# Loading the first FFN's weights as f32 through staging slots, with ScalarE and VectorE doing the cast

## What is computed

```python
def swiglu(h, w_gate, w_up, w_down):
    return (jax.nn.silu(h @ w_gate) * (h @ w_up)) @ w_down

x = x + 0.5 * swiglu(rmsnorm(x, ffn1_norm), ffn1_w_gate, ffn1_w_up, ffn1_w_down)
h = rmsnorm(x, mix_norm)
...
x = x + merged @ w_out
x = x + 0.5 * swiglu(rmsnorm(x, ffn2_norm), ffn2_w_gate, ffn2_w_up, ffn2_w_down)
```

## Time and profile before

| | |
|---|---|
| median of 3 runs | 3398.79 us |
| profiled execution | 3418.33 us |
| span on its slowest core (core 6) | 3416.7 us |
| spans of the 8 cores | 3388.2 to 3416.7 us |
| TensorE busy | 3075.1 us, 90% |
| VectorE, ScalarE, GpSimd busy | 33%, 26%, 20% |
| first matmul | 130.47 us |
| DMA moved | 403 MB, 118 GB/s on average |

### The profile page before, as it was taken

How to read it: one execution, slowest core, us unless ns; L and a number is a source line. 1 busy time by engine, 2 the same in 40 slices (tenths; PEclk the granted TensorE clock), 3 DMA queues, 4 the chain that set the end, 5 groups by cost and what they waited for, 6 DMA issues and landing times.

```text
span 3416.7 us, 41299 instructions; the slowest of 8 cores (3388.2 to 3416.7 us)
## 1 busy us (share of the span) xinstructions
PE 3075.1 (90%) x14115; PEld 1406.9 (41%) x14400; DVE 1115.5 (33%) x1555; ACT 893.4 (26%) x1733; POOL 690.1 (20%) x1149
## 2 busy tenths in 40 slices
PE   0487999898899879998999989999999999999999
PEld 0243444343344434443444444444444444444444
DVE  1111221121122464535365545453422221222111
ACT  0111111111111245363644353646221111111100
POOL 2000000000000463535244535342110000000000
PEclk9998999999999999999999999999999999999999
DMA  9743532632631648767578877656773212321111
GB/s 176 144 61 77 114 50 65 119 53 67 127 63 70 160 101 197 154 170 153 145 176 208 176 180 167 169 139 171 242 229 87 72 41 61 87 71 41 49 50 37
DMA packets 335976, 403.05 MB, mean 118 GB/s; under 512 B 208800, under 2 KB 217120, under 8 KB 335008
## 3 DMA queue, kind: packets, MB, share of 16 engines
q1 hardware_dynamic: 323248, 347.27, 39.2%
q0 software_dynamic: 12528, 53.12, 11.4%
HBM read 355.38 MB, written 86.64 MB: 129 GB/s over the span
## 4 chain that ended last, share of the span: by engine, by line
PE 74%; DMA 14%; SPq 3%; DVE 3%; POOL 3%; issue 2%; ACT 1%; another core or an unknown queue 0%; ACTq 0%; DVEq 0%; POOLq 0%
PE banks L698 74%; SPq L841 2%; DMA x1s<-axr_99 2%; DMA axr_98<-x 2%; DMA xin_68<-x 1%; DMA hT_66<-xn_71 1%; DMA xin_69<-x1s 1%; DMA x1s<-axr_98 1%; POOL hr L1030 1%; DMA KT<-kf 1%; DMA xin_69<-x 1%; POOL qf L1041 1%; SPq L869 1%; DMA QT_115<-qf 1%; DMA axr_99<-x 1%
## 5 line engine op out<-in xcount | busy, mean ns | idle before, releaser
L834 POOL TENSOR_SCALAR ssq<-ssq 128x1 f32<-128x1 f32 x96 | 19.4, 202 | 1645.5 <-ACT xn_70 L832 1544.1
L698 PE MATMUL banks<-awd,aact 128*128 128x512 bf16 x1380 | 304.4, 379 | 1.5
L698 PE MATMUL banks<-cwd,cact 128*128 128x512 bf16 x1380 | 303.7, 379 | 1.5
L698 PEld LDWEIGHTS banks<-cwd,cact 128*128 128x128 bf16 x1408 | 137.7, 98 | 166.2
L698 PEld LDWEIGHTS banks<-awd,aact 128*128 128x128 bf16 x1408 | 137.8, 98 | 165.6
L883 ACT ACTIVATE asg_94<-banks 128x512 f32<-128x512 f32 x88 | 52.6, 597 | 512.8 <-PE banks L698 499.7
L698 PE MATMUL banks<-hT_66,agu_72 128*128 128x512 bf16 x64 | 21.9, 518 | 166.4 <-DMA hT_66<-xn_71 130.5
L883 ACT ACTIVATE csg_161<-banks 128x512 f32<-128x512 f32 x88 | 52.5, 597 | 434.0 <-PE banks L698 433.9
L698 PE MATMUL banks<-QT_115,KT 128*128 128x512 bf16 (+3 forms) x377 | 131.5, 355 | 16.2 <-ACT pt_118 L1096 5.2
L1096 ACT ACTIVATE pt_118<-banks 128x512 bf16<-128x512 f32 (+2 forms) x216 | 115.9, 537 | 87.6 <-PE banks L698 84.0
L885 DVE TENSOR_TENSOR cact<-csg_162,banks 128x512 bf16<-128x512 f32 x88 | 60.5, 688 | 238.4 <-PE banks L698 224.6
(11 more groups left out here) (406 smaller groups left out, 5497.7 us busy)
## 6 DMA issues: line engine op xcount, KB each, us to landing
wms<-ws POOLq DMA_DIRECT2D x33, 512.0 KB, 6.7
ring_129<-wms SPq DMA_DIRECT2D x52, 256.0 KB, 4.3
ring_131<-wms SPq DMA_DIRECT2D x51, 256.0 KB, 3.8
ring_133<-wms SPq DMA_DIRECT2D x51, 256.0 KB, 4.0
ring_135<-wms SPq DMA_DIRECT2D x51, 256.0 KB, 4.1
ring_137<-wms SPq DMA_DIRECT2D x51, 256.0 KB, 3.8
ring_130<-wms SPq DMA_DIRECT2D x39, 256.0 KB, 4.7
ring_132<-wms SPq DMA_DIRECT2D x39, 256.0 KB, 4.9
```

The source lines that it names most:

```text
L698: fns.append(lambda e, o_=o_, l_=l_, r_=r_, st=st, sp_=sp_: e.matmul(o_, lhsT=l_, rhs=r_, start=st, stop=sp_))
L834: yield op("pool", lambda e, i=i: e.tensor_scalar(out=ssq.t[:, i, 1:2], in0=ssq.t[:, i, 0:1], scalar1=EPS, scalar2=1.0, op0=ALU.add, op1=A ...
```

## The change

FFN1's weights are loaded as plain f32 from SyncE's queue. A gate/up piece (1 MB) goes into one of five staging slots `stg` (`astg`), which lie where the down weights will be; ScalarE casts the gate half into `agu`, VectorE the up half. From the third piece on a load is released in the planning when a tile's transpose has been planned. The down weights follow as 22 slices of 0.5 MB, through the four residual slots, cast by ScalarE and VectorE in turn. Dependences are finer: gate matmuls wait for the gate half, a slice of the down weights is a dependence of its own. For group 0 of FFN1 the down projection runs slice by slice over all 8 PSUM banks (4 tiles x 2 halves) instead of bank by bank. The residual has four slots (two `xr`, two `dscr`), in both FFNs; group 0's tiles are loaded after the last weight slice, and each further tile right after the store that frees its slot, for the next group. `DMA_RATE` of the planner goes from 320 to 340.

```diff
-DMA_RATE = 320.0
+DMA_RATE = 340.0
...
+    NSTG = 5
...
+        f.stg = []
+        if tag == "a":
+            for i in range(NSTG):
+                f.stg.append(mk(f"{tag}stg{i}", [2, 1024], F32, a + 8192 * i, 2))
+                for dp in f.stg[-1].d:
+                    dp.until = "f1.stg"
+            commit_regs(f.stg)
+        f.wd = mk(f"{tag}wd", [NFC, D], BF16, a, NFC)
...
+        f.xr = [(b.t[:], b.d) for b in xr] + [(b.t[:, 0:D], b.d) for b in dscr]
...
     def load_w1():
         yield Wait(lambda: "seta" in flags)
-        for (nm, dst, dd, si) in fpieces("f1", f1):
-            off, F = woff[nm]
-            yield dma("pool", s_w[si], lambda e, dst=dst, off=off, F=F: e.dma_start(out=dst, in_=ws_d[:, off:off + F]),
-                      [], dd, 128 * F * 2)
...
+        for c in range(NFC):
+            yield Wait(lambda c=c: c < 2 or f"f1.t.0.{min(c - 2, TPG - 1)}" in flags)
+            off, F = woff[f"f1gu{c}"]
+            sb = f1.stg[c % NSTG]
+            yield dma("sp", s_w[c % NSTG], lambda e, sb=sb, off=off, F=F: e.dma_start(
+                out=sb.t[:].rearrange("p a n -> p (a n)"), in_=ws_d[:, off:off + F]), [], sb.d, 128 * F * 4)
+            gu = f1.gu[c]
+            yield op("act", lambda e, sb=sb, gu=gu: e.activation(out=gu.t[:, 0].rearrange("p k m -> p (k m)"), in_=sb.t[:, 0, :], func=AF.Copy),
+                     [sb.d[0]], [gu.d[0]], c_act(1024))
+            yield op("dve", lambda e, sb=sb, gu=gu: e.tensor_copy(out=gu.t[:, 1].rearrange("p k m -> p (k m)"), in_=sb.t[:, 1, :]),
+                     [sb.d[1]], [gu.d[1]], c_dve(1024, 2))
+        yield Do(lambda: flags.add("f1.stg"))
+        yield Wait(lambda: "rope" in flags)
+        for k in range(NFC):
+            off = woff[f"f1d{k // DPIECE}"][0] + 1024 * (k % DPIECE)
+            ap, dd = f1.xr[k % 4]
+            yield dma("sp", s_w[NSTG + k % 4], lambda e, ap=ap, off=off: e.dma_start(out=ap, in_=ws_d[:, off:off + 1024]),
+                      [], dd, 128 * 4096)
+            if k % 2 == 0:
+                yield op("act", lambda e, ap=ap, k=k: e.activation(out=f1.wd.t[:, k, :], in_=ap, func=AF.Copy), dd, [f1.wd.d[k]], c_act(1024))
+            else:
+                yield op("dve", lambda e, ap=ap, k=k: e.tensor_copy(out=f1.wd.t[:, k, :], in_=ap), dd, [f1.wd.d[k]], c_dve(1024, 2))
...
     def ffn_stream(tag, f, src_d, srcdep, dst_d, dstdep, bnk, start, xgate):
...
-                if c in (14, 18):
-                    yield ld(0 if c == 14 else 1)
...
+            outer = tag == "f1" and g == 0
+            if outer:
+                yield pend
+                pend = None
+                for kc in range(NFC):
+                    lst = [(bk(2 * tt + hf), f.act.t[:, kc, tt * 128:(tt + 1) * 128], f.wd.t[:, kc, hf * 512:(hf + 1) * 512],
+                            kc == 0, kc == NFC - 1) for tt in range(TPG) for hf in range(2)]
+                    yield mms(lst, [f.wd.d[kc], f.act.d[kc]], d_bank, 512)
+            if g == 0:
+                yield Wait(xgate)
+                for tt in range(TPG):
+                    yield ld(0, tt)
...
-                if tt + 2 < TPG:
-                    yield ld(tt + 2)
+                if g + 1 < NG:
+                    yield ld(g + 1, tt)
```

More of the change, by code:

```diff
@@ L580, in ffn_bufs @@
         a = f.act.end
-        f.wd = mk(f"{tag}wd", [NFC, D], BF16, a, NFC // DPIECE)
+        f.stg = []
[6 more added lines that the diff above has]
+        f.wd = mk(f"{tag}wd", [NFC, D], BF16, a, NFC)
         a = f.wd.end
-        f.xr = []
+        xr = []
         for i in range(2):
-            f.xr.append(mk(f"{tag}xr{i}", [D], F32, a, 2))
-            a = f.xr[-1].end
+            xr.append(mk(f"{tag}xr{i}", [D], F32, a, 2))
+            a = xr[-1].end
         assert a <= HI, (a, HI)
-        f.all = f.gu + f.sg + [f.act] + [f.wd] + f.xr
+        f.all = f.gu + f.sg + [f.act] + [f.wd] + xr
+        f.xr = [(b.t[:], b.d) for b in xr] + [(b.t[:, 0:D], b.d) for b in dscr]
         return f
@@ L671, in build_program @@
     s_tx = [fw.new_dma_sem(f"tx{i}") for i in range(2)]
-    s_xr = [fw.new_dma_sem(f"xr{i}") for i in range(2)]
-    s_xs = [fw.new_dma_sem(f"xs{i}") for i in range(2)]
+    s_xr = [fw.new_dma_sem(f"xr{i}") for i in range(4)]
+    s_xs = [fw.new_dma_sem(f"xs{i}") for i in range(4)]
     s_xo = [fw.new_dma_sem(f"xo{i}") for i in range(6)]
@@ L677, in build_program @@
     s_wl = [fw.new_dma_sem(f"wl{i}") for i in range(2)]
-    s_w = [fw.new_dma_sem(f"w{i}") for i in range(NFC + NFC // DPIECE)]
+    s_w = [fw.new_dma_sem(f"w{i}") for i in range(NSTG + 4)]
     s_v = [fw.new_dma_sem(f"v{i}") for i in range(NFC + NFC // DPIECE)]
@@ L768, in load_w1 @@
         yield Wait(lambda: "seta" in flags)
[L769 to L773 removed]
+        for c in range(NFC):
[20 more added lines that the diff above has]
+                yield op("dve", lambda e, ap=ap, k=k: e.tensor_copy(out=f1.wd.t[:, k, :], in_=ap), dd, [f1.wd.d[k]], c_dve(1024, 2))
+        yield Do(lambda: flags.add("w1.done"))
     def load_w2():
@@ L842, in norm_stream, with ffn_stream @@
                       xn[i].d, [d_hT[g % 2][tt]], 128 * D * 2)
+            yield Do(lambda n_=f"{tag}.t.{g}.{tt}": flags.add(n_))
             if tt == TPG - 1:
                 yield Do(lambda n_=f"{tag}.n.{g}": flags.add(n_))
-    def ffn_stream(tag, f, src_d, srcdep, dst_d, dstdep, bnk, start):
+    def ffn_stream(tag, f, src_d, srcdep, dst_d, dstdep, bnk, start, xgate):
         yield Wait(start)
@@ L854, in nb, with ld @@
             return b
+        def ld(g, tt):
+            r0 = g * G + tt * 128
+            ap, dd = f.xr[tt]
+            return dma("sp", s_xr[tt], lambda e: e.dma_start(out=ap, in_=src_d[r0:r0 + 128, :]), srcdep(g, tt), dd, 128 * D * 4)
         for g in range(NG):
@@ L860, in ffn_stream @@
             pend = None
[L861 to L870, removed]
             for c in range(NFC):
@@ L896, in ffn_stream @@
                     cut = 20 if pend is not None else NFC
-                    yield mms(lst[:cut], [f.wd.d, f.act.d[:cut]], [d_bank[b0]], 512)
+                    if not outer:
+                        yield mms(lst[:cut], [f.wd.d, f.act.d[:cut]], [d_bank[b0]], 512)
                     if pend is not None:
```

27 lines of the change are left out of this document (14 added, 13 removed).

## The result

The changed kernel takes 3274.9 us (median of three runs; the kernel before, in the same comparison, 3400.3): a ratio of 0.9642, 95% interval [0.9607, 0.9677]. Two repeats gave 0.9603 [0.9589, 0.9617] and 0.9622 [0.9601, 0.9642]. Faster, as forecast, by 122 to 136 us; 3257 had been predicted, with a range of 3215 to 3305.

The account below looks back on a forecast made before the run. TensorE is busy 3075 of 3416.7 us; its idle lies before the first matmul and behind FFN1's residual add. Group 7 starts at 889 instead of 1031.1, the rest 0: 142 off 3398.8 gives 3257, range 3215 to 3305.

Parts of the forecast that it names:

- Start of TensorE: Group 0 of FFN1: first matmul at 41 us (36 to 57) instead of 130.5, after 9.4 MB and four transposes.
- Gate/up: Group 0 of FFN1: 22 steps of 3.45 us, not held up by weights or casts, ending at T = 119.
- First down: Group 0's down projection: one wait, about 36 us, for slices behind a transpose beside GpSimd's casts; group 1 at 199.
- Groups 1 to 6: FFN1: with four residual slots the add waits for nothing, 115 us a group; group 7 at 889, not 1031.1.
- rival (c): FFN1: SyncE's four store-then-load pairs of a group each catch the casts; seven groups grow by 32 us: 3481; chance 0.03.
- (b): FFN1's groups keep their waits, with hT or a store late instead of x; 63 us come back: 3320; chance 0.13.
- (a): First down does not wait, slices 20 and 21 arriving before the casts; group 1 36 us earlier: 3221; chance 0.11.
- (d): Staging a fifth under the start's pace: step 4.1 us, gate/up 14 us more, start 10 more: 3281; chance 0.09.
- The rest: Behind FFN1: FFN2 gains nothing; DMA_RATE reorders the mixing stage, bounded at 20 us either way, taken as 0.
- The sum: Whole kernel: 1031.1 - 889 = 142 us gained up to group 7, leaving 3257 from the median.

Follow-up runs that it names:

- the run with fewer bytes ahead: Only the first weight piece loaded ahead of the fourth transpose, against the kernel with GpSimd's first casts a group later: 0.9499 of the kernel before, 3248 us.
- the run with the order alone: Last slice loads put ahead of group 2's norms and transposes, GpSimd's casts kept near their old time, against the changed kernel: 3286.4 and 3291.4 us.

## Why the prediction was right, and where not

- *Start of TensorE, 41 us (36 to 57):* 38.7 to 42.6, mean 40.5. That the start is the bytes ahead of the fourth transpose was the right reason: with four pieces fewer it came 10 us earlier. The terms of the sum were less exact than the sum: on core 2 the fourth transpose is issued at 33.57, where the sum has 35 to 38, although the bytes up to then move at 275 GB/s (8.14 MB from 4 to 33.6 us) and not at 375; and it takes 8.9 us to land, not some 3. That they cancel is luck.
- *Gate/up at 3.45 us a step, T = 119:* 3.45, and T = 121.4 on core 2 (117.95 + 3.45). Weights and casts stay hidden.
- *First down, 36 us of waits, group 1 at T + 80 = 199:* 10.40 + 8.70 + 12.00 + 4.93 = 36.0, four waits where one was forecast, and 202.05 = T + 80.6; on the other cores they add up to 35 to 38. The size is right and the cause (the casts) too: without them beside it the wait is gone. The mechanism in the text is not. The last transpose "stands ahead of the loads of slices 20 and 21 and, as in the earlier trace rows, cannot land before the casts end at about T + 64": these loads wait for its issue, 26.84 us, not for its landing, which came at 189.3; in return each plain load is itself stretched from 7 or 8 us to 21.6 to 36.7, so that slices 18 and 19, which stood ahead of it, were late too. One error made the chain too long, the other too short. Both chains end a few us behind the casts (190.7 and 192.0 against about 188), which is why the time comes out; that it fits to 0.6 us is luck. With the slices first, the text's mechanism would have removed the wait; it moved to the residual loads and the norm's loads.
- *Groups 1 to 6 at 115:* 115.5, then 113.9; 685.7 us on the mean of the cores. Two slots bring 751 back, so this term, 66 us (752 - 686), is the four slots'. A store is followed by its load 4 us later (x1s at 198.68, the load into its slot at 203.01), so rival (c) had no ground, nor had (b).
- *Rivals (a) and (d):* (a) fails with the 36.0 us of waits. (d) fails with the steps of 3.45 us, at 328 GB/s on core 2 from 42.6 to 122.4 us. Its price has a slip: a fifth under 308 is 246 GB/s, which makes 4.3 us a step, not 4.1, and about 3288, not 3281; it stays inside the range.
- *The rest, 0 (20 either way):* +7 to +13 us in the three profiled executions. This is the term that was mis-sized. That it is the order of the mixing stage is supported by 10.7 us in the kernel before with nothing but DMA_RATE changed; which instructions there lose the time stays open.
- *The sum:* 142 up to group 7 was 143.0 and 141.5; less the rest, 133 and 129 by the traces. The two profiled executions differ by 3418.3 - 3284.4 = 134; the three ratios make it 122, 136 and 129. The forecast of 3257 took 142 off a median of 3398.8; in the four later sets that kernel took 3418 to 3421.

The parts are worth, each taken away alone: residual slots 70 us (3352 - 3282), staging 53, the slice order 18 to 50 (its runs spread most; group 1 comes 28 us later). And 34 us (3282 - 3248) lay in one line of the cast schedule.

The rule that spoke against a gain in bandwidth held: the Trainium skill, "DMA: Bandwidth & Descriptors", section "Issuing engines are not separate DMA queues", says that another issuing engine saves little more than the time of the issue. These traces agree: with the engines full the staged loads run at 328 GB/s in gate/up of the changed kernel and at 309 in the run with fewer bytes ahead, the start of the kernel before at 308 (40 MB read in 130 us). What the change gained at the start is that TensorE begins after a part of the bytes.

## What to carry to other kernels

When a load is stretched by a burst on another queue, putting it earlier in its own queue can just pass the stretch to the next load, as here; move the burst to a time when nothing near its end is waited for. After an edit that frees one resource, look for the next thing that sets the same moment (here the casts, then the bytes) before counting the gain twice. A planner's cost figure is a change of its own: test it alone, and expect each edit to draw a new order worth a few microseconds either way.

## What the runs showed of the hardware that was not expected

Beside GpSimd's casts, which hold 73 to 81% of the engines with some 500 to 580 packets in 50 us, every kind of transfer on SyncE's queue is stretched: a load of 512 KB from 7 or 8 to 37 us, a store from 4 to 47.7, a transpose from 7 to 48.7. An estimate from the rows of the queues says where the time goes. In the share of the engines that it gets, SyncE's queue moves 264 GB/s beside the casts (3.29 MB in 24.9% of 50 us), or 231 in the run with the order alone (3.03 MB in 26.2%), and 292 without them (13.37 MB in 91.6%). So its packets are a tenth to a fifth slower; what it lacks above all is its share. How the engines choose between the queues no run shows. SyncE itself is held while it issues: 23 to 36 us over the cores for that one transpose, 26.84 on core 2, where its 96 issues of transposes have a median of 1.23 and the next longest takes 8.9; and in the run with the order alone a plain load too (SyncE in order of time, core 5: start, us, what):

```profile
174.19 23.76 SPq L844 DMA_DIRECT2D xin<-x  x1
```

That is 23.76 us for one load of x, against 0.46 and 0.33 us for the loads of slices 18 and 19 in the rows of the changed kernel above, and 2.71 and 4.13 for the two loads right behind the held transpose. So a transfer can be late before it is issued at all; the profile then shows SyncE in the issue ahead of it, not in a wait.
